# A two-layer diffusion backbone: the new x is scaled by tokens and turned by TensorE transposes, and ScalarE takes three of eight shifts

## The reference

```python
def rmsnorm(t, gain):
    tf = t.astype(jnp.float32)
    tf = tf * lax.rsqrt(jnp.mean(tf * tf, axis=-1, keepdims=True) + NORM_EPS)
    return tf.astype(t.dtype) * gain

ux = rmsnorm(x, g[0]) * (1 + scale) + shift        # scale, shift: vectors over the 2048 channels
x = x + gate * rmsnorm(sublayer(ux), g[1])
```

## Time and profile before

| | us |
|---|---|
| median of 3 runs | 2294.62 (2293.51 to 2298.75) |
| the profiled execution | 2290.86 |
| its span from first to last instruction | 2289.1 |
| TensorE busy | 2213.6 (97% of the span) |
| VectorE busy | 1660.9 (73%) |
| ScalarE busy | 1002.0 (44%) |
| GpSimd busy | 98.8 (4%) |

### The profile page before, as it was taken

How to read it: one execution, slowest core, us unless ns; L and a number is a source line. 1 busy time by engine, 2 the same in 40 slices (tenths; PEclk the granted TensorE clock), 3 DMA queues, 4 the chain that set the end, 5 groups by cost and what they waited for, 6 DMA issues and landing times.

```text
span 2289.1 us, 31071 instructions
## 1 busy us (share of the span) xinstructions
PE 2213.6 (97%) x11423; PEld 1825.0 (80%) x11423; DVE 1660.9 (73%) x1799; ACT 1002.0 (44%) x1233; POOL 98.8 (4%) x32
## 2 busy tenths in 40 slices
PE   7899998899999999999989999999999999999998
PEld 3478567788888888888868888878888888888887
DVE  0266666798788888888989889988887554655565
ACT  3164543544344344344444444454444443443443
POOL 0000000001010110110101101100011000000000
PEclk9899999999999999999999999999999999999999
DMA  9966977688888878889867888895887666666654
GB/s 374 357 219 234 369 263 261 233 264 271 296 278 287 295 257 302 288 269 312 300 203 276 286 294 282 275 317 180 288 288 252 193 194 184 182 194 193 204 190 150
DMA packets 253898, 592.67 MB, mean 259 GB/s; under 512 B 18082, under 2 KB 18610, under 8 KB 253234
## 3 DMA queue, kind: packets, MB, share of 16 engines
q1 hardware_dynamic: 253746, 590.63, 76.7%
HBM read 588.46 MB, written 2.10 MB: 258 GB/s over the span
## 4 chain that ended last, share of the span: by engine, by line
PE 87%; DVE 5%; DMA 4%; issue 2%; ACT 1%; SPq 0%; DVEq 0%; ACTq 0%
PE ps L517 30%; PE ps L518 15%; PE ps L580 11%; PE ps L581 11%; PE ps L582 11%; PE ps L544 2%; DMA early<-in_w_mod_dram 2%; PE ps L475 1%; DMA raw<-in_mlp_w_dram 1%; DVE wlo L1208 1%; DVE acc L1218 1%; ACT whi L878 1%; DMA mraw<-in_w_mod_dram 1%; PE ps L672 1%; PE ps L703 0%
## 5 line engine op out<-in xcount | busy, mean ns | idle before, releaser
L1208 DVE TENSOR_TENSOR wlo<-raw,whi 128x1024 fp32r<-128x1024 f32 x712 | 901.9, 1271 | 435.8 <-ACT whi L878 434.3
L878 ACT ACTIVATE whi<-raw 128x1024 fp32r<-128x1024 f32 x712 | 751.4, 1058 | 962.5 <-PE ps L582 384.5
L517 PE MATMUL ps<-u,whi 128*128 128x512 f32 x2944 | 1037.7, 397 | 7.8 <-DVE wlo L1208 4.7
L518 PE MATMUL ps<-u,wlo 128*128 128x256 f32 x2944 | 824.5, 280 | 1.4 <-issue 1.4
L517 PEld LDWEIGHTS ps<-u,whi 128*128 128x128 f32 x2944 | 553.6, 188 | 144.9 <-issue 6.7
L518 PEld LDWEIGHTS ps<-u,wlo 128*128 128x128 f32 x2944 | 556.4, 189 | 1.9 <-issue 1.8
L580 PE MATMUL ps<-whi,h 128*128 128x512 f32 x1216 | 475.9, 391 | 5.0 <-DVE wlo L1208 4.9
L581 PE MATMUL ps<-wlo,h 128*128 128x512 f32 x1216 | 474.0, 390 | 0.0
L582 PE MATMUL ps<-whi,h 128*128 128x512 f32 x1216 | 473.8, 390 | 0.0
L1218 DVE SCALAR_TENSOR_TENSOR acc<-mraw,cs,acc 128x1024 f32<-128x1024 f32 x240 | 311.2, 1297 | 6.4 <-DMA mraw<-in_w_mod_dram 6.1
L580 PEld LDWEIGHTS ps<-whi,h 128*128 128x128 f32 x1216 | 228.9, 188 | 55.8 <-DVE wlo L1208 7.7
(11 more groups left out here) (191 smaller groups left out, 1266.1 us busy)
## 6 DMA issues: line engine op xcount, KB each, us to landing
raw<-in_mlp_w_dram SPq DMA_DIRECT2D x512, 512.0 KB, 4.6
mraw<-in_w_mod_dram SPq DMA_DIRECT2D x272, 512.0 KB, 5.6
early<-in_w_mod_dram SPq DMA_DIRECT2D x96, 512.0 KB, 6.6
raw<-in_conv_w_in_dram SPq DMA_DIRECT2D x96, 512.0 KB, 5.6
raw<-in_att_w_in_dram SPq DMA_DIRECT2D x40, 512.0 KB, 5.1
raw<-in_att_w_out_dram SPq DMA_DIRECT2D x32, 512.0 KB, 5.9
raw<-in_conv_w_out_dram SPq DMA_DIRECT2D x32, 512.0 KB, 6.1
raw<-in_w_mod_dram SPq DMA_DIRECT2D x16, 512.0 KB, 6.8
```

The source lines that it names most:

```text
L517: pe.matmul(bank, whi[:, s % SLOTS, cols], src[:, k, :], start=(k == 0), stop=False)
L518: last = pe.matmul(bank[:, 0:T], wlo[:, s % SLOTS, cols], src[:, k, 0:T], start=False, stop=(k == KC - 1))
L878: act.activation(whi[:, s, :], raw[:, s, :], ACT.Copy).then_inc(hi_ready, 1)
L1208: dve.tensor_tensor(wlo[:, s, :], raw[:, s, :], whi[:, s, :], ALU.subtract).then_inc(lo_ready, 1)
```

## The change

In the norm, DVE no longer writes a diagonal. It multiplies the first 512 channels of x by `r_x` by tokens into `yt` (for the second token half in two instructions of 256 channels), and ACT does the same for the three other groups of 512 channels (`scale_x`, with `r_x` as the scale of an ACT copy). TensorE turns blocks of `yt` by its transpose operation with the identity. Pair 2 moves from ahead of slab 0 to ahead of slab 1, where pair 3 is turned too. ACT takes the scaling and shifting by channel for pairs 1, 3 and 5 (`ACT_PAIRS`), DVE keeps the other five. Both engines' lists at a boundary are reordered: on DVE an x piece now stands between shift and low, the other x piece behind the `lo`, and the x pieces of group 1 stand behind shift 0. On ACT `hi` of slabs 2 and 3 stand behind `scale_x(1)`, and `high` 3 and 5 behind `scale_x` and a `hi`. The semaphores `first_scaled`, `x_scaled` and `act_shifted` are new; `u_shifted` counts five shifts for each boundary (`shifts_through`).

```diff
+ACT_PAIRS = (1, 3, 5)
...
+
+        def shifts_through(j, b):
+
+            return 8 + 5 * j + sum(1 for p in range(b + 1) if p not in ACT_PAIRS)
...
@@ -808,26 +814,32 @@
                 def turn_half(b, a):
                     for c in range(2):
                         k = 2 * b + c
-                        last = pe.matmul(ps[:, turn_bank(slot, b), c * T + a * P:c * T + (a + 1) * P],
-                                         x[:, a, k * P:(k + 1) * P], diag[:, a, :], start=True, stop=True)
+                        last = pe.transpose(ps[:, turn_bank(slot, b), c * T + a * P:c * T + (a + 1) * P],
+                                            yt[:, a, k * P:(k + 1) * P], ident)
                     if a:
                         last.then_inc(u_t, 1)
...
                 def turn(b):
                     if b % 2 == 0:
-                        pe.wait_ge(x_step, 8 * j + b + 2)
-                    if b >= 4:
-                        pe.wait_ge(u_shifted, 8 * (j + 1) + b - 3)
-                    turn_pair(x, 0, b, turn_bank(slot, b), u_t)
+                        pe.wait_ge(x_scaled, 6 * j + b)
+                    if b in (5, 7):
+                        pe.wait_ge(act_shifted, 3 * j + (b - 3) // 2)
+                    elif b >= 4:
+                        pe.wait_ge(u_shifted, shifts_through(j, b - 4))
+                    turn_half(b, 0)
+                    turn_half(b, 1)
 
                 def ahead(s):
                     if s == 0:
-                        for a in range(2):
-                            pe.wait_ge(diag_ready, 3 + 2 * j + a)
-                            pe.wait_ge(x_step, 8 * j + a + 1)
-                            turn_half(0, a)
-                            turn_half(1, a)
+                        pe.wait_ge(first_scaled, 3 * j + 1)
+                        turn_half(0, 0)
+                        turn_half(1, 0)
+                        for b in range(2):
+                            pe.wait_ge(first_scaled, 3 * j + 2 + b)
+                            turn_half(b, 1)
+                    elif s == 1:
                         turn(2)
+                        turn(3)
                     elif s < SL - 2:
                         turn(s + 2)
...
+            def boundary(j, w0, shift):
...
+                slot = (w0 // SL + 1) % 2
+
+                def shifted(b):
+                    act.wait_ge(u_t, 8 * j + b + 1)
+                    if b >= 2:
+                        act.wait_ge(u_ready, 8 * (j + 1) + b - 1)
+                    for c in range(2):
+                        k = 2 * b + c
+                        last = act.activation(mt[b % 2][:, c, :], two_tiles(turn_bank(slot, b))[:, c, :], ACT.Identity,
+                                              scale=der[:, k:k + 1], bias=vt[:, shift + k:shift + k + 1])
+                    last.then_inc(act_shifted, 1)
+
+                def high(b):
+                    if b in ACT_PAIRS:
+                        act.wait_ge(act_shifted, 3 * j + (b + 1) // 2)
+                    else:
+                        act.wait_ge(u_shifted, shifts_through(j, b))
+                    act.activation(u[:, 2 * b:2 * b + 2, 0:T], mt[b % 2], ACT.Copy).then_inc(u_hi, 1)
+
+                def scale_x(g):
+                    for a in range(2):
+                        cols = slice(g * GW, (g + 1) * GW)
+                        act.wait_ge(rstd_ready, 4 + 4 * j + 2 * a)
+                        act.wait_ge(x_step, 8 * j + 2 * g + a + 1)
+                        act.activation(yt[:, a, cols], x[:, a, cols], ACT.Copy, scale=r_x[:, a:a + 1]
+                                       ).then_inc(x_scaled, 1)
+
+                act.wait_ge(gs_ready, j + 1)
+                high(0)
+                shifted(1)
+                high(1)
+                scale_x(1)
                 hi(w0 + 2, 2)
                 hi(w0 + 3, 3)
-                for b in range(PAIRS):
-                    pair_high(8 * (j + 1) + b, mt[b % 2])
-                    if 2 <= b < 6:
-                        hi(w0 + 2 + b, (2 + b) % SLOTS)
+                for b in (2, 4):
+                    high(b)
+                    shifted(b + 1)
+                    scale_x(b // 2 + 1)
+                    hi(w0 + b + 2, (b + 2) % SLOTS)
+                    high(b + 1)
+                    hi(w0 + b + 3, (b + 3) % SLOTS)
+                high(6)
+                high(7)
...
-                dve.tensor_scalar(diag[:, a, :], ident, r_x[:, col], None, ALU.mult).then_inc(diag_ready, 1)
+                dve.wait_ge(x_step, 8 * j + a + 1)
+                for first, wide in ((0, GW),) if a == 0 else ((0, T), (T, T)):
+                    dve.tensor_scalar(yt[:, a, first:first + wide], x[:, a, first:first + wide], r_x[:, col], None,
+                                      ALU.mult).then_inc(first_scaled, 1)
...
             def boundary(j, scale, gain, shift, w0):
 
-                for a in range(2):
-                    x_piece(j, 1, a)
...
                 def low(b):
-                    dve.wait_ge(u_shifted, n0 + b + 1)
+                    if b in ACT_PAIRS:
+                        dve.wait_ge(act_shifted, 3 * j + (b + 1) // 2)
+                    else:
+                        dve.wait_ge(u_shifted, shifts_through(j, b))
                     pair_low(n0 + b, mt[b % 2])
-                shifted(0)
-                for b in range(PAIRS):
-                    if b + 1 < PAIRS:
-                        shifted(b + 1)
+                for b in range(0, PAIRS, 2):
+                    shifted(b)
+                    if b < 6:
+                        x_piece(j, b // 2 + 1, 0)
                     low(b)
-                    if b < 7:
-                        lo(w0 + 1 + b, (1 + b) % SLOTS)
-                    if b in (1, 3):
-                        for a in range(2):
-                            x_piece(j, b // 2 + 2, a)
+                    if b:
+                        lo(w0 + b, b % SLOTS)
+                    if b < 6:
+                        x_piece(j, b // 2 + 1, 1)
+                    else:
+                        shifted(7)
+                    low(b + 1)
+                    lo(w0 + b + 1, (b + 1) % SLOTS)
```

More of the change, by code:

```diff
@@ L212, in backbone_program @@
             "ysq_ready", "yg_ready", "zsq_ready", "xz_ready", "sums_ready", "n_step", "x_step"))
+        first_scaled, x_scaled, act_shifted = sem("first_scaled"), sem("x_scaled"), sem("act_shifted")
         rows_landed, gs_ready, u_shifted, u_hi, u_ready, n_sums = (sem(n) for n in (
@@ L1129, in out_stage @@
                             row_squares(j, pg0 + i, i)
-            def boundary(j, w0):
+            def boundary(j, w0, shift):
[27 more added lines that the diff above has]
+                scale_x(1)
                 hi(w0 + 2, 2)
                 hi(w0 + 3, 3)
-                for b in range(PAIRS):
-                    pair_high(8 * (j + 1) + b, mt[b % 2])
-                    if 2 <= b < 6:
-                        hi(w0 + 2 + b, (2 + b) % SLOTS)
+                for b in (2, 4):
[7 more added lines that the diff above has]
+                high(7)
             def mlp(l):
@@ L1179, in _ @@
             out_stage(0, PG_WO, slab_of(PG_MLP[0]))
-            boundary(0, slab_of(PG_MLP[0]))
+            boundary(0, slab_of(PG_MLP[0]), 3 * KC)
             mlp(0)
-            boundary(1, slab_of(PG_CONV))
+            boundary(1, slab_of(PG_CONV), 6 * KC)
             def v_high(t):
@@ L1198, in _ @@
             out_stage(2, PG_CO, slab_of(PG_MLP[1]))
-            boundary(2, slab_of(PG_MLP[1]))
+            boundary(2, slab_of(PG_MLP[1]), 9 * KC)
             mlp(1)
```

## The result

The changed kernel has a median of 2312.12 us over 8 runs (2304.75 to 2317.52), the kernel before 2299.17 over 8 runs on the same chip (2292.87 to 2303.19). The ratio is 1.0061, with a 95% interval from 1.0045 to 1.0077: slower, by 14.0 us on 2294.62 where 10.8 were forecast. The profiled execution took 2312.80. A second comparison of the same kernel gave 1.0053 [1.0029, 1.0077]; one execution of each kernel in it was far slower than all others (10287 and 2762 us) and is left out of the ratio.

The account below looks back on a forecast made before the run. TensorE, with 87% of the last chain, was taken to bound the kernel. Three boundaries at 3.6 us each add 10.8 to the median of 2294.62, giving 2305.4 us; the 8-in-10 range was 2298 to 2314.

Parts of the forecast that it names:

- Slab 0: At each boundary, its start was put at 458.92 instead of 459.54, 0.6 us earlier.
- The two new forms of ScalarE: ScalarE's 128x512 copy with a scale, put at 725 ns, and its 128x256 shift with scale and bias, 587 ns.
- The stalls: TensorE's waits ahead of pairs 4 and 6 (2.0 and 1.6 us) and slabs 6 and 7 (0.2 and 0.7), 4.5 together.
- The whole walk at full clock: The three engines' lists followed through a boundary without clock loss: next group at 488.6, 2.2 us later than 486.38.
- Rival (c): At pair 4's wait for ScalarE's scaled x: no stalls, TensorE keeps its savings, 6.2 us saved in all, 2288.4; chance 0.08.
- The clock: At slab 0's start: 1.2 GHz for 2.9 us more, slab ending 1.4 us later; bounds no loss or 3.4 us longer.
- The rule cited from the Trainium skill: On TensorE ahead of slab 0: transposes don't count as busy for the clock as products do; next group at 489.96, otherwise 488.6.
- Rival (b): Behind the 2.0 and 1.6 us stalls: clock falls for 3.4 us each, 4.8 to 9.6 us more, 2310 to 2315; chance 0.10.
- Costed at nothing: After the boundary, at slab 11: VectorE keeps 1.7 us of slack, so no cost; 1 us a boundary if that cover is gone.
- boundary 2 is alike to 0.01 us: Boundary 2 matches boundary 1's distance from turn to slab 0, so 3.6 us was taken for each of three alike boundaries.
- The sum: Over the three boundaries: 489.96 less 486.38, 3.6 us each, 10.8 in all.
- more than 1 us outside the boundaries: A sign that the forecast is wrong: time outside the boundaries changes by more than 1 us.

Follow-up runs that it names:

- keep_warm: The changed kernel with idle TensorE products added at each boundary, 7 behind the first token half's transposes and 4 behind the second's; ratio to the kernel before 1.0019.
- x_before_lo: The changed kernel with the second x piece of channel groups 2 and 3 moved ahead of `lo` 2 and `lo` 4 on VectorE; ratio to the kernel before 1.0036.
- x_early: The changed kernel with the same instructions reordered at the boundary, x pieces and `scale_x` far ahead of need; ratio to the kernel before 0.9973.
- x_early_warm: x_early with the idle products of keep_warm added; 2283.09 us, ratio to the kernel before 0.9955.
- x_early_warm_tr: x_early_warm with 28 and 16 idle transposes in place of the 7 and 4 idle products; ratio to the kernel before 0.9969.
- x_early_products: x_early with the blocks of scaled x turned by fp32 products with the identity in place of transposes; ratio to the kernel before 1.0019.
- x_early_dve: x_early without ScalarE's shifts, VectorE doing all eight, with an early order of its own; ratio to the kernel before 0.9990.

## Why the prediction was right, and where its terms were off

**Slab 0.** 3.80 us after the reciprocal was forecast, 3.66 to 3.91 measured. The two new forms of ScalarE were priced at 725 and 587 ns. The groups of the changed kernel:

```profile
L817 PE MATMUL ps<-tab,y 128*128 128x128 f32 x96 | 15.9, 297 | 21.2 <-DVE y L1684 13.5 <-ACT y L1170 7.5
...
L1170 ACT ACTIVATE y<-x,st 128x512 f32<-128x512 f32 x18 | 12.6, 716 | 5.7 <-DVE x L1655 5.7
...
L1154 ACT ACTIVATE fq<-ps,vt,der 128x256 f32<-128x256 f32 x18 | 9.1, 554 | 1.1 <-PE ps L817 1.1
```

**The stalls.** Forecast 2.0, 1.6, 0.2 and 0.7; with the full clock all along (keep_warm, boundary 3) they are 1.95, 1.69, 0.26 and 0.46. The whole walk at full clock was put at 2.2 us over the kernel before and measures 2.7 (33.99 - 31.25). The forecast's own terms (4.5 less 0.6, less 5 x 0.38, plus 0.43) make 2.4, not 2.2. Part of the rest lies between the stalls: slab 2 starts 5.38 us after slab 1, where 2.86 of slab, 1.95 of stall and 0.43 of transposes make 5.24. x_before_lo shows that `lo` 2 ahead of the x piece makes 1.18 of the 1.95, and x_early that the rest is order too. Rival (c) would have come true with such an order. The one x piece's place alone isn't enough: x_before_lo is still slower than the kernel before.

**The clock.** The low stretch did reach into slab 0, but for 4.2, 4.2 and 6.1 us from its start and not 2.9, within the bound that the forecast gave (3.4 later). By the changed kernel less keep_warm it costs 1.9, 2.2 and 3.1 us a boundary, where 1.4 was the term: 7.1 for 4.2, the term of the sum that was mis-sized most. x_early agrees: against x_early_warm's 28.88 it has 30.48 with 3.0 us of low clock from slab 0 on and 31.73 with 6.0, about half a microsecond lost for each low one.

The rule cited from the Trainium skill ("TensorE: Matmul & The Clock Gate", Part 4 (PE-mode transpose)), that transposes don't count as busy in the same way, isn't borne out: x_early_warm_tr keeps the clock at 1.00 with transposes as TensorE's only work from the old group's end to slab 0. Nor did products in their place help (x_early_products). What the rows show is how little TensorE does there: at boundary 1 of the changed kernel 0.70 us of transposes after a wait of 4.31, and then nothing for 2.51. Filling both waits, with either kind of work, removes the low stretch.

**Rival (b)**, falls behind the stalls, happened in part, at boundaries 1 and 2. It priced each fall at 1.6 us; behind pair 4 a fall cost nothing, since the wait ahead of pair 6 went with it.

**"Costed at nothing".** The step that failed, by 3.3 us for nothing, is the one on what comes after the boundary: 1.7 us of slack, 1 us if the cover is gone, looked for at slab 11. At boundary 2 it was gone at slab 8. The kernel before, GpSimd's, VectorE's and TensorE's timelines:

```profile
1211.98 6.11 POOL L1845 PARTITION_ALL_REDUCE red<-acc  x1 [102.28 <-DVE u L1378]
```
```profile
1212.00 5.59 DVE L1208 TENSOR_TENSOR wlo<-raw,whi 128x1024 fp32r<-128x1024 f32 x1
```
```profile
1217.74 0.47 PE L517 MATMUL ps<-u,whi 128*128 128x512 f32 x1 [0.81 <-DVE wlo L1208]
```

and the changed kernel:

```profile
1228.10 6.95 POOL L1901 PARTITION_ALL_REDUCE red<-acc  x1 [109.33 <-DVE u L1427]
```
```profile
1229.14 5.41 DVE L1257 TENSOR_TENSOR wlo<-raw,whi 128x1024 fp32r<-128x1024 f32 x1
```

GpSimd starts its sum over partitions when the boundary's last `low` is done, and the `lo` of slab 8 beside it takes 5.4 to 5.6 us instead of 1.22. Before, VectorE was far enough ahead that TensorE stood 0.81 us for it. Now the boundary's last `low` is done later, so this `lo` ends later, at 1234.55; TensorE stands 2.49, and in the profiled execution the clock falls after it for 3.4 us (from 1234.7), with no later wait to absorb that: 1.6 more. The other kernels of the late order stand 2.5 too (2.47 to 2.53), x_early 0.43. This fits what the Trainium skill says in "GPSIMD Engine Reference", "1. Specifications", that GpSimd shares its SBUF interfaces with VectorE and that they contend when VectorE's instruction has two SBUF inputs, as `lo` has; the section gives no size. The all-reduce and TensorE's 0.81 us were in the trace of before, and boundary 1, where the walk was made and TensorE "never waits", has no such instruction; "boundary 2 is alike to 0.01 us" was read up to slab 0 only.

**The sum**, in us over three boundaries to the group after the next: the walk 8.2 (6.6 forecast), slab 0's clock 7.1 (4.2), slab 8's wait at boundary 2 1.7 (0), the fall behind it 1.6 (0), and 0.4 for slower slabs behind boundary 3 (see below); 19.0 in all, against 10.8.

**What stays open.** The profiles give +19.0 and +17.3, the ratios +14.0 [10.3, 17.7] and +12.2 [6.7, 17.7]. In 9 of the 12 profiles other than those of the kernel before, the boundaries' sum lies 3.7 to 7.8 us above what the ratio gives. The profiled executions of before (2290.86 and about 2290) are below its medians of 2295 to 2299, and an offset in what all are compared with would fit; no run settles it.

The time outside the boundaries ranges from 2126 to 2136 us between the profiled executions, and much of that arises where the programs are the same. The first transposes or turns of boundary 1 start at 448.82 us in x_early and at 454.84 in x_early_dve, at 450.66 in the kernel before and at 454.33 in the changed one. Two things vary from one execution to the next. One is how long the clock is low up to there: 48 us in x_early and in before, 61 in x_early_dve. The other is the pace of the slabs at a granted clock of 1.00: 2.77 us from slab to slab in one stretch, 2.83 in another (in the changed kernel 497.48 to 500.25 behind boundary 1, and 1619.55 to 1622.37 behind boundary 3). No run shows what sets either. The forecast took more than 1 us outside the boundaries as a sign of being wrong; the changed kernel has 3.0 more, but it was 3.7 behind before the change acts at all, so that sign says nothing here.

So the forecast's 10.8 stands within the interval of the ratio while its terms were low by 8 in the profiles. The stalls and the late clock that it named are what came, but slab 8's wait came too; that the total lies as close as it does is in part luck.

## What to carry to other kernels

When work is handed from one engine to the next and back, walk the chain through every list: an instruction that only stands in front, like the 1.22 us `lo` ahead of an x piece, is paid for at the far end, and the same instructions in another order made a slower kernel a faster one. Ask what clock the first dense work finds after each wait you create or lengthen, and walk the boundary that differs (here the one with GpSimd's all-reduce) too, up to where the cover is used up.

## What the runs showed of the hardware that was not expected

- VectorE's subtraction of 128x1024 took 5.41 to 5.59 us beside GpSimd's all-reduce, against 1.22 alone. Only one instruction pays: beside each of the 13 all-reduces of the kernel before a single VectorE instruction is long (8 of its 712 `lo`, one sum of the modulation at 5.56, four others at 4.5), and a `lo` that starts beside the same all-reduce after it takes 1.21 again.
- Stalls of 1.9 to 2.65 us ahead of pair 4, between slabs at 1.00, were followed by 3.4 us at 0.50 in 9 of 12 boundaries (four profiles); those of 0.77 to 0.82 in none of 3. Of the stalls of 2.5 ahead of slab 8, x_before_lo's was followed by none. Within one kernel it happened at one boundary and not at the next.
- Idle transposes keep the granted clock up as well as idle products: in both kernels it was 1.00 across all three boundaries.
- At a granted clock of 1.00 with TensorE never idle, slabs follow each other at 2.77 us in some stretches of an execution and at 2.83 in others, with the kernel before as with the changed one.
